# A hand-written order of early weight pieces: 31 visits become 29, and a visit runs on over the end of its period

## What is computed

```
shift, scale, gate = c @ W_ada + b_ada            # W_ada is 2048 x 6144
h = RMSNorm_pre(x) * (1 + scale) + shift          # needs shift and scale of every channel
p = h @ W_in                                      # W_in is 2048 x 11328; columns for q, kv-latent (ckv),
                                                  # rope key, diff q/k/v (vd), four gate column blocks
...                                               # two attentions, merge, W_out, second norm, residual
```

## Time and profile before

| what | value |
|---|---|
| median of 3 runs | 766.87 us (766.79 to 767.28) |
| profiled execution | 767.12 us, span 765.3 us |
| PE busy | 749.6 us, 98% of the span |
| DVE busy | 562.4 us, 73% |
| ACT busy | 420.0 us, 55% |
| start of the first piece on PE | 23.87 us |
| first piece behind the 70 (rope key) | 219.65 us |

### The profile page before, as it was taken

How to read it: one execution, slowest core, us unless ns; L and a number is a source line. 1 busy time by engine, 2 the same in 40 slices (tenths; PEclk the granted TensorE clock), 3 DMA queues, 4 the chain that set the end, 5 groups by cost and what they waited for, 6 DMA issues and landing times.

```text
span 765.3 us, 10103 instructions
## 1 busy us (share of the span) xinstructions
PE 749.6 (98%) x3679; PEld 625.4 (82%) x3679; DVE 562.4 (73%) x824; ACT 420.0 (55%) x638; POOL 21.6 (3%) x94
## 2 busy tenths in 40 slices
PE   5999999999999999999999999999999999999997
PEld 5887788888888988888888888888888888888885
DVE  4899999889868579888887778676554556465554
ACT  4588777765567554544545565655444444444441
POOL 2000000000000000000000000011100000000000
PEclk9999999999999999999999999999999999999999
DMA  9999999998674789888886575655566656567642
GB/s 338 395 392 395 380 390 338 354 371 287 186 225 126 211 280 311 284 273 282 290 291 194 162 218 184 165 169 165 179 180 194 193 177 205 186 207 246 223 156 110
DMA packets 132556, 189.72 MB, mean 248 GB/s; under 512 B 10325, under 2 KB 68122, under 8 KB 132250
## 3 DMA queue, kind: packets, MB, share of 16 engines
q1 hardware_dynamic: 132240, 188.77, 75.5%
q10 hardware_dynamic: 266, 0.30, 0.1%
HBM read 185.90 MB, written 2.10 MB: 246 GB/s over the span
## 4 chain that ended last, share of the span: by engine, by line
PE 90%; ACT 2%; DVE 2%; DMA 2%; SPq 2%; issue 1%; DVEq 0%; POOLq 0%; POOL 0%; ACTq 0%
PE ps L1901 17%; PE ps L1903 17%; PE ps L1902 16%; PE ps L1891 13%; PE ps L1860 8%; PE ps L1877 7%; PE ps L1863 4%; DMA w_raw<-in_w_in 2%; SPq L525 2%; ACT w_both L1029 1%; PE ps L1698 1%; DVE ada_acc L1309 1%; PE ps L1683 1%; PE ps L1713 1%; DVE w_both L1558 1%
## 5 line engine op out<-in xcount | busy, mean ns | idle before, releaser
L1558 DVE TENSOR_TENSOR w_both<-w_raw,w_both 128x1024 fp32r<-128x1024 f32 x247 | 300.5, 1222 | 160.1 <-ACT w_both L1029 158.8
L1029 ACT CAST w_both<-w_raw 128x1024 fp32r<-128x1024 f32 x248 | 258.9, 1049 | 246.3 <-PE ps L1903 183.7
L1891 PE MATMUL ps<-w_both,h_both 128*128 128x512 f32 x560 | 138.8, 390 | 0.0
L1891 PEld LDWEIGHTS ps<-w_both,h_both 128*128 128x128 f32 x560 | 105.0, 188 | 22.8 <-DVE w_both L1558 0.7
L1901 PE MATMUL ps<-w_both,h_both 128*128 128x512 f32 x296 | 116.8, 395 | 0.0
L1903 PE MATMUL ps<-w_both,h_both 128*128 128x512 f32 x296 | 115.4, 390 | 0.0
L1902 PE MATMUL ps<-w_both,h_both 128*128 128x512 f32 x296 | 115.2, 389 | 0.0
L1877 PE MATMUL ps<-w_both,h_both 128*128 128x512 f32 x280 | 76.0, 393 | 0.9 <-ACT h_both L980 0.6
L1309 DVE SCALAR_TENSOR_TENSOR ada_acc<-ada_ring,cols,ada_acc 128x512 f32<-128x512 f32 x98 | 69.6, 745 | 0.5
L1901 PEld LDWEIGHTS ps<-w_both,h_both 128*128 128x128 f32 x296 | 55.6, 188 | 12.7 <-issue 1.7
L1903 PEld LDWEIGHTS ps<-w_both,h_both 128*128 128x128 f32 x296 | 55.5, 188 | 11.7
(11 more groups left out here) (265 smaller groups left out, 847.1 us busy)
## 6 DMA issues: line engine op xcount, KB each, us to landing
w_raw<-in_w_in SPq DMA_DIRECT2D x177, 512.0 KB, 4.5
ada_ring<-in_w_ada SPq DMA_DIRECT2D x128, 256.0 KB, 6.4
gate_ring<-in_w_ada SPq DMA_DIRECT2D x32, 512.0 KB, 5.2
w_raw<-in_w_out SPq DMA_DIRECT2D x32, 512.0 KB, 3.7
w_raw<-in_w_o_mla SPq DMA_DIRECT2D x16, 512.0 KB, 4.0
w_raw<-in_w_o_diff SPq DMA_DIRECT2D x16, 512.0 KB, 4.0
w_raw<-in_w_ukv SPq DMA_DIRECT2D x16, 256.0 KB, 3.4
x_tok<-in_x SPq DMA_DIRECT2D x2, 1024.0 KB, 6.0
```

The lines of the kernel that those rows point to most:

```text
L1029: act.copy(w_hi[:, p % RING, :], w_raw[:, p % RING, :]).then_inc(hi_done, 1)
L1558: dve.tensor_tensor(w_lo[:, p % RING, :], w_raw[:, p % RING, :], w_hi[:, p % RING, :].bitcast(F32), ALU.subtract).then_inc(lo_done, 1)
L1891: ins = mm(ps[:, b0 + t, :], lhsT=side[:, 2 * i + r, t * P:(t + 1) * P], rhs=w[:, p % RING, r * CH:(r + 1) * CH], start=False, stop=last a ...
```

## The change

Only the list of the plan changes. It has 29 visits in place of 31. From period 2 on, a period starts with `0`, so the visit behind each turn carries on over what was the period's end and is the one that opens the new pair; other visits are longer or shorter to fit, some turns move by one place, and what is seeded and what is added follows. The number of pieces (70), of copies out (23) and of seeds (15) stays; 8 visits that were added become 6.

```diff
-    [(("ckv", 0), (0, 1)), 0, (("vd", 0), (1,)), (("vd", 1), (1,)), 1, TURN, (("gate", 3), (1,)), (("gate", 0), (1,))],
-    [(("gate", 1), (1, 2)), 0, (("gate", 2), (1, 2)), 1, TURN, (("q", 2), (1, 2))],
-    [(("vd", 0), (2, 3)), 0, (("vd", 1), (2, 3)), 1, TURN, (("gate", 0), (2, 3)), (("gate", 3), (2,))],
-    [(("ckv", 0), (2, 3, 4)), 0, (("q", 2), (3, 4)), 1, TURN, (("gate", 1), (3, 4))],
-    [(("gate", 3), (3, 4, 5)), 0, (("gate", 2), (3, 4, 5)), 1, TURN, (("vd", 0), (4, 5))],
-    [(("vd", 1), (4, 5, 6)), 0, (("gate", 0), (4, 5, 6)), 1, TURN, (("q", 2), (5, 6))],
-    [(("ckv", 0), (5, 6, 7)), 0, (("q", 2), (7,)), 1, (("gate", 0), (7,))],
+    [(("ckv", 0), (0, 1)), 0, (("vd", 0), (1,)), (("vd", 1), (1,)), 1, TURN, (("gate", 3), (1,)), (("gate", 1), (1, 2))],
+    [0, (("gate", 2), (1, 2)), (("gate", 0), (1,)), 1, TURN, (("q", 2), (1, 2, 3))],
+    [0, (("vd", 0), (2, 3)), (("vd", 1), (2, 3)), 1, TURN, (("gate", 3), (2, 3, 4))],
+    [0, (("ckv", 0), (2, 3, 4)), (("gate", 0), (2,)), 1, TURN, (("gate", 2), (3, 4, 5))],
+    [0, (("gate", 1), (3, 4)), (("gate", 0), (3, 4, 5)), 1, TURN, (("vd", 0), (4, 5, 6))],
+    [0, (("vd", 1), (4, 5, 6)), (("q", 2), (4, 5, 6)), 1, TURN, (("ckv", 0), (5, 6, 7))],
+    [0, (("q", 2), (7,)), 1, (("gate", 0), (6, 7))],
 ]
...
-SEEDED = [8, 9, 10, 12, 13, 14, 15, 16, 17, 19, 20, 21, 22, 23, 24]
+SEEDED = [v for v in range(8, 24) if v != 11]
```

## The result

The changed kernel takes **772.62 us** in the median (772.48 to 773.03, 5 runs) against 767.15 us (766.79 to 767.44, 5 runs) for the kernel before: ratio 1.0072, 95% interval 1.0060 to 1.0083. That is 5.5 us slower. The forecast was 771.6 us, +4.7. Its profiled execution has a span of 770.8 us.

The account below looks back on a forecast made before the run. PE, busy 98% of the span, was taken as the bound. New waits for h of 6.25 us less 1.53 us of old waits gave +4.7, 771.8 us profiled, 771.6 us as median; range 768.8 to 774.8 us.

Parts of the forecast that it names:

- T + 7.74: At each opening, T being the turn's start on PE: when PE wants h's low part if the high part is on time.
- the sum: Behind turns 2 to 7: new waits for h of 6.25 us less 1.53 us of old losses, +4.7 us.
- The old losses of 1.5 us: PE's waits behind turn 2 in the kernel before, mostly between turns 2 and 3; forecast to go.
- Costed at nothing: DVE additions, other seeds, W_ada rows, SP loads and later stages: priced at 0 us; later stages only take over the delay.
- The forecast of the rope key: Behind the stage of 70 places: the rope key starts near 224.3 in the changed kernel.
- the median 0.25 us below the profiled execution: Whole kernel: the profiled time of 771.8 us was lowered by 0.25 to a forecast median of 771.6 us.
- The lower bound (+2.7): Behind turns 3 to 7: DVE takes up the low part some 0.4 us sooner each, 2 us less.
- The upper bound (+6.6): Low parts behind turns 6 and 7 as late as turn 3's, and restarts costing 0.2 us rather than 0.1.
- A delay that feeds on itself: Rival: a late opening delays copy, seed and next visit; five middle turns lose another 1 us each, +9.7, 776.6 us; 8%.
- The clock: Rival: clock drops to 1.2 GHz for about a piece behind each of six openings, 16.3 us more, 788 us; 3%.
- The rival of the other sign: Behind every turn the low part comes by T + 7.68, no opening waits, 1.5 us won, 765.3 us median; 5%.

Follow-up runs that it names:

- e5: Changed kernel with two spare ACT copies of 512 elements ahead of the full part of h behind turns 3 to 7; 776.59 us.
- e11: Changed kernel with two spare ACT copies of 512 elements behind the full part of h, for turns 3 to 7; 772.74 us.
- e1: Changed kernel with high and full part of h made together two places behind each turn, ahead of that place's copies and seeds; 769.23 us.
- e9: Changed kernel with the edit of e1 for turns 2 to 7 alone, turn 1 as it was; 767.96 us.
- e10: e9 with the late jobs behind the rope key in the order gate 1, gate 2, vd 0, gate 3, vd 1; 767.35 us.
- e2: Changed kernel with only the high part of h moved ahead of copies and seeds two places behind each turn; 774.27 us.
- e12: e10 with visit 12's seed a place later, gate 0 pairs 1 and 2 between turns 2 and 3, one visit fewer between turns 4 and 5; 766.04 us.
- e8: Changed kernel with gate 0 pair 2 moved behind turn 4, so pair 4 opens a piece later, that visit added instead of seeded; 772.77 us.

## Why the prediction was right

**The mechanism was right.** Behind turns 3 to 7 the changed kernel asks for the low part of h at T + 7.74 (behind turn 2 later, since it waits for the high part first), and it gets it where the trace of before said. The losses against the sum, turn by turn: turn 2 2.53 (predicted 2.50), turn 3 1.00 (1.00), turn 4 0.99 (0.96), turn 5 0.99 (0.96), turn 6's opening 0.54 (0.52), turn 7 0.31 (0.31). The old losses of 1.5 us went as forecast: turn 3 no longer waits for DVE, and it starts at 90.39 (forecast 90.4). e5 with e11 shows the cause, and e1 and e9 show it from the other side.

**What the sum missed** are 0.2 + 0.46 of the 5.5 us; another 0.1 is spread over the turns. The step was "Costed at nothing". It let the later stages only take over the delay, but the new plan leaves one pair of vd 0 and three of gate 3 for them instead of two and two, which moves the late jobs by a place against DVE's rope work: 0.46 us (e10 takes it back). It also said that DVE has no part in PE's pace except before turn 3, and passed over the addition whose banks turn 7 uses: 0.2 us, by its rows; that was not tried by itself. The forecast of the rope key, 224.3, was 0.3 early. The sum also set the median 0.25 us below the profiled execution, from three runs; with five the kernel before has 767.15 against 767.12, so that step was chance, and it made the forecast a little lower than the 771.8 that the mechanism gives.

**The bounds and the rivals.** The lower bound (+2.7) took DVE to be quicker with the low part than before; it wasn't. The upper bound (+6.6) held. A delay that feeds on itself did not show: behind each wait the other seeds were in time. The clock stayed at its higher level (1.00, 2.4 GHz) in every window of the changed kernel, with waits of up to 1.31 us, and in e2's trace with one of 2.31 us; e2's three longer runs (0.996) leave open whether it always does. By the Trainium skill, "TensorE: Matmul & The Clock Gate", section "A second HAM failure mode: psum-queue depth-cycling", frequent tiny pauses can make the clock go back and forth. In the changed kernel's trace the waits at the six openings, 23 us and more from one opening to the next, did not bring that about. The rival of the other sign, a chain that is there in time, came true only where the chain itself was made earlier, as in e9 and e12; it doesn't come with the plan.

## What to carry to other kernels

When an order of work is rearranged so that a consumer asks sooner, work out for each hand-over when it asks and when the producer delivers, both counted from the same event. The producer's chain can be read from the trace of before, even where nothing waits for it yet. Look at everything that the list feeds, also what it leaves over for the stages behind it, and change the producer's place together with the consumer's: alone, the new order cost 5.5 us here and the earlier chain 5.1 (2.0 of it behind turn 1, which the later runs leave as it was), and both together with small repairs won 1.

## What was not expected

- In e2 the profiled execution and the other runs of one kernel differ by 1.6 to 1.9 us (772.65, and 774.25 to 774.57), the longer ones at a mean clock of 0.996.
- Taking a wait away twice returned less than its length, because the wait had been giving another engine time: 0.96 us at turn 4 came back as 0.64 at turn 5 (e8), and turn 3 went back to waiting for DVE (0.36 us) as soon as turn 2's wait was gone (e9).
